# Input projection of a diffusion backbone step: kept row parts, weight splits moved from GpSimd, and conditioning vectors computed on TensorE between projection steps

## What is computed

```python
mod = silu(c) @ w_mod + b_mod            # c for latent rows, c_ctx for context rows; w_mod 2048 x 12288
sh1, sc1, g1, sh2, sc2, g2 = split(mod, 6)                 # six vectors of 2048, for each of the two kinds of row
h = rmsnorm(x, norm1_g) * (1 + sc1) + sh1
p = h @ w_in                                               # 2048 x 4608
dq, dk, dv, gq, gk, gv = split(p)                          # differential heads, grouped-query heads
gq, gk = rmsnorm(gq, qn_g), rmsnorm(gk, kn_g)              # then rotary positions on latent rows of dq, dk, gq, gk
o = concat(diff_attention(dq, dk, dv), gqa(gq, gk, gv))    # latent rows read 128 cached rows too
x = x + g1 * (o @ w_out)                                   # 2048 x 2048
h2 = rmsnorm(x, norm2_g) * (1 + sc2) + sh2
x = x + g2 * experts(h2)                                   # 16 experts, top-k rows each, SwiGLU 2048 -> 1024 -> 2048
y = rmsnorm(x, final_norm_g)
```

## Time and profile before

| | us |
|---|---|
| median of 3 runs (2669.41 to 2671.88) | 2670.93 |
| the profiled execution, its own time | 2671.9 |
| its span, first to last instruction | 2669.8 |
| conditioning | 0 to 106.6 |
| turn-over | 106.6 to 119.9 |
| input projection | 119.9 to 876.4 |
| values' loads, until the first score | 876.4 to 882.6 |
| attention | 882.6 to 1205.6 |
| start of the output projection | 1205.6 to 1211.1 |
| output projection | 1211.1 to 1459.5 |
| norm, routing, gathering | 1459.5 to 1533.3 |
| experts | 1533.3 to 2629.7 |
| end | 2629.7 to 2669.8 |

### The profile page before, as it was taken

The page is one execution under the profiler, slowest core; times in us unless marked ns, Lnnn a source line. Parts: engine busy times, 40 slices in busy tenths (PEclk is TensorE's granted clock), DMA queues, the critical chain, the costliest instruction groups (busy, mean ns, idle before and its releaser), DMA issues.

```text
span 2669.8 us, 28206 instructions
## 1 busy us (share of the span) xinstructions
PE 2252.4 (84%) x10506; PEld 1573.5 (59%) x10506; DVE 2007.6 (75%) x1696; ACT 1226.3 (46%) x1293; POOL 873.8 (33%) x396
## 2 busy tenths in 40 slices
PE   3777866887788788878999299999999999999994
PEld 0256645665566556657777266666666666666662
DVE  1177899998983477774322599999999998889895
ACT  1233322232223333323210277777777776666773
POOL 1297967899996000000000001111111111222221
PEclk8698988898988899978999599999999999999997
DMA  9753433346431200004212899999999999999996
GB/s 380 292 189 122 143 128 133 136 143 213 173 126 64 97 1 1 1 1 160 79 64 89 303 354 376 380 381 379 382 380 384 384 384 384 380 379 379 378 390 235
DMA packets 207807, 623.78 MB, mean 234 GB/s; under 512 B 10745, under 2 KB 12281, under 8 KB 172233
## 3 DMA queue, kind: packets, MB, share of 16 engines
q1 hardware_dynamic: 194880, 557.88, 56.1%
q0 software_dynamic: 6496, 35.51, 4.9%
q10 hardware_dynamic: 6352, 29.36, 2.9%
HBM read 593.15 MB, written 29.62 MB: 233 GB/s over the span
## 4 chain that ended last, share of the span: by engine, by line
PE 56%; DVE 21%; DMA 9%; POOL 8%; issue 3%; ACT 2%; SPq 0%; ACTq 0%; DVEq 0%; POOLq 0%; PEldq 0%
PE ps L505 16%; PE ps L506 16%; PE ps L507 16%; DVE arena L1451 7%; POOL B_x_lo L1226 4%; POOL B_w_lo L1227 3%; DMA arena<-in_w_mod 3%; DMA arena<-in_w_expert_down 3%; DVE arena L1415 2%; PE ps L766 2%; DVE mx L1465 2%; DVE arena L1417 2%; PE ps L732 2%; DVE arena L1410 1%; ACT arena L1065 1%
## 5 line engine op out<-in xcount | busy, mean ns | idle before, releaser
L1165 ACT ACTIVATE E_w_hi<-arena 128x2048 fp32r<-128x2048 f32 x384 | 735.9, 1917 | 282.2 <-PE ps L507 170.4
L1655 DVE TENSOR_TENSOR E_w_lo<-arena,E_w_hi 128x2048 fp32r<-128x2048 f32 x256 | 579.4, 2287 | 71.5 <-ACT E_w_hi L1165 70.3
L1304 POOL DMA_INDIRECT acc_d<-arena,idxC x16 | 181.9, 11371 | 764.1 <-DVE arena L1698 764.1
L1451 DVE SCALAR_TENSOR_TENSOR arena<-arena,cT 128x2048 f32<-128x2048 f32 x120 | 393.9, 3321 | 38.2 <-DMA arena<-in_w_mod 33.4
L505 PE MATMUL ps<-E_w_hi,E_xsT_hi 128*80 128x512 f32 x1024 | 405.9, 396 | 13.1 <-DVE E_w_lo L1655 13.1
L1226 POOL TENSOR_TENSOR B_x_lo<-arena,B_x_hi 128x640 fp32r<-128x640 f32 x144 | 362.5, 2520 | 165.3 <-ACT B_w_hi L965 151.4
L506 PE MATMUL ps<-E_w_hi,E_xsT_lo 128*80 128x512 f32 x1024 | 403.4, 394 | 0.0
L1655 DVE TENSOR_TENSOR E_w_lo_late<-arena,E_w_hi 128x2048 fp32r<-128x2048 f32 x128 | 291.9, 2287 | 14.6 <-ACT E_w_hi L1165 13.8
L507 PE MATMUL ps<-E_w_lo,E_xsT_hi 128*80 128x512 f32 x768 | 300.0, 391 | 0.0
L507 PE MATMUL ps<-B_w_lo,B_x_hi 128*128 128x512 f32 x720 | 293.2, 407 | 0.0
L505 PE MATMUL ps<-B_w_hi,B_x_hi 128*128 128x512 f32 x360 | 154.3, 429 | 106.2 <-POOL B_w_lo L1227 105.4
(11 more groups left out here) (215 smaller groups left out, 3755.0 us busy)
## 6 DMA issues: line engine op xcount, KB each, us to landing
arena<-in_w_expert_gate SPq DMA_DIRECT2D x128, 1024.0 KB, 14.2
arena<-in_w_expert_up SPq DMA_DIRECT2D x128, 1024.0 KB, 14.4
arena<-in_w_expert_down SPq DMA_DIRECT2D x128, 1024.0 KB, 17.4
arena<-in_w_mod SPq DMA_DIRECT2D x96, 1024.0 KB, 5.6
arena<-in_w_in SPq DMA_DIRECT2D x36, 1024.0 KB, 5.7
arena<-in_w_out SPq DMA_DIRECT2D x16, 1024.0 KB, 5.0
arena<-in_x_sample ACTq DMA_DIRECT2D x8, 1024.0 KB, 11.7
acc_d<-arena POOLq DMA_DIRECT2D x1, 5120.0 KB, 18.9
```

Of the source, the lines that this page charges most:

```text
L1165: act.activation(split_e(j)[0][:, :], at(slot_e(j), D), ACT.Copy).then_inc(xw_hi, 1)
L1304: pool.indirect_dma_start(acc_d[:, :], bass.IndirectOffsetOnAxis(ap=idxC[:, e:e + 1], axis=0), xrow_out[0:CAP, :], None, compute_op=ALU.ad ...
L1451: ins = dve.scalar_tensor_tensor(out=maccs[m][v], in0=w, scalar=cT[:, k, v:v + 1], in1=maccs[m][v], op0=ALU.mult, op1=ALU.add)
L1655: dve.tensor_tensor(w_lo[:, :], at(slot_e(j), D), w_hi[:, :].bitcast(F32), ALU.subtract).then_inc(xw_lo, 1)
```

## The change

ORDER becomes 8, 2, 3, 4, 0, 1, 6, 7, 5. The row parts `x_hi` and `x_lo` of all sixteen channel pieces are computed once and stay in memory ("xsplit": four activations on ScalarE, L1045, two of which apply scale and shift with rounding and two in place, and one subtraction on VectorE, L1442). The weights are split in halves of a chunk (128x1024, two steps; 72 halves): `w_hi` by ScalarE (L1038) in a ring of three, `w_lo` by VectorE (L1438) in place of the raw weights. GpSimd computes nothing there but two small powers; it issues DMAs. All 96 chunks of `w_mod` go through TensorE (L721, `cT` padded with zeros to 32 columns): 32 in the first stage, where c and c_ctx are now the first transfers of SyncE's queue and the row transposes (L706, L709) and their plain copies (L1022) stand between the chunks, and 64 between the steps of the projection, where `MOD_AT` puts them, through a ring of two. The sums over partitions, `selv`, the accumulators and "cols2" are gone; a finished vector is copied out of its bank (L1031) and turned by four transposes (L697).

The V loads go to SyncE's queue, issued after step 11 of the last block. `x` is loaded again once the scores are done. The output projection is split by halves too (`HI_D` = 3 halves, before 3 chunks), and the residual of a block comes before the next split on VectorE. Eleven of the first twelve expert chunks are issued ahead of the wait for `acc_stored`, before eight. The memory layout changes with all this. Attention, routing and the expert loop are as before.

```diff
-ORDER = [8, 6, 7, 2, 3, 4, 0, 1, 5]
+ORDER = [8, 2, 3, 4, 0, 1, 6, 7, 5]
...
-MOD_PACE = [(2, 3, 3, 3), (0, 2, 3, 3), (0, 1, 3, 3), (0, 1, 3, 3), (0, 2, 3, 3), (1, 2, 2, 3), (2, 2, 3, 3), (0, 1, 2, 2)]
+TEN, NINE = (0, 2, 3, 5, 6, 8, 10, 11, 13, 14), (0, 2, 4, 5, 7, 9, 11, 12, 14)
+MOD_AT = [(1, 3, 5, 7, 9, 11, 13, 15), TEN, TEN, NINE, NINE, NINE, NINE, (), ()]
...
+                elif kind == "mod":
+                    n = step[1]
+                    where, s, fill = mod_slot(n)
+                    mi, k = n // KC, n % KC
+                    if n == 0:
+                        pe.wait_ge(c_ready, 1)
+                    elif k == 0:
+                        pe.wait_ge(mod_copied, mi)
+                    pe.wait_ge(mod_landed[s], 16 * fill)
+                    w = at(where, 4, NB)
                     for c in range(4):
-                        mm = pe.matmul(bank(4 * m + c)[32 * c:32 * c + 2, :], cT[:, k, :], w[:, c, :], start=(k == 0),
-                                       stop=(k == KC - 1))
+                        mm = pe.matmul(bank(5)[32 * c:32 * (c + 1), :], cT[:, k, :], w[:, c, :], start=(k == 0),
+                                       stop=(k == KC - 1), skip_group_check=True)
+                    mm.then_inc(mod_used if k < KC - 1 else mod_done, 1)
                 elif kind == "projk":
...
-                    pe.wait_ge(pb_lo, n_k + 1)
+                    if k % 2 == 0:
+                        pe.wait_ge(w_lo_ready, u + 1)
+                    if o == 0:
+                        pe.wait_ge(x_lo_ready, k + 1)
...
+                elif kind == "split":
+                    u = step[1]
+                    raw, w_hi, _ = half_b(u)
+                    if u >= HI_B:
+                        after_products(act, (u - HI_B) // 8, 2 * ((u - HI_B) % 8) + 1)
+                    act.wait_ge(w_landed[u // 2 % RING_B], 16 * (u // 2 // RING_B + 1))
+                    act.activation(w_hi, raw, ACT.Copy).then_inc(w_hi_ready, 1)
+                elif kind == "xsplit":
+                    k = step[1]
+                    if k == 0:
+                        act.wait_ge(A1_ready, 1)
+                    for dst in (parts_B["x_hi"][k], xT[:, k, :]):
+                        for v, cols in ((0, slice(0, LAT)), (1, slice(LAT, TOK))):
+                            ins = act.activation(dst[:, cols], xT[:, k, cols], ACT.Identity, bias=modT[:, 0, v, k:k + 1],
+                                                 scale=A1[:, v, k:k + 1])
+                    ins.then_inc(x_hi_ready, 1)
...
-            def low_parts(n):
-
-                (x, w), (x_hi, w_hi), (x_lo, w_lo) = split_b(n)
-                pool.wait_ge(pb_hi, n + 1)
-                pool.tensor_tensor(x_lo, x, x_hi.bitcast(F32), ALU.subtract)
-                pool.tensor_tensor(w_lo, w, w_hi.bitcast(F32), ALU.subtract).then_inc(pb_lo, 1)
...
+                elif kind == "split":
+                    u = step[1]
+                    raw, w_hi, w_lo = half_b(u)
+                    dve.wait_ge(w_hi_ready, u + 1)
+                    dve.tensor_tensor(w_lo, raw, w_hi.bitcast(F32), ALU.subtract).then_inc(w_lo_ready, 1)
```

897 lines of the change are left out of this document (430 added, 467 removed).

## The result

The changed kernel takes 2478.91 us (median of four runs, 2475.09 to 2480.68) for 2671.4 of the kernel before: a ratio of 0.928, with an interval of 0.926 to 0.930. That is 192.5 us less, where 174 were forecast, and lies inside the range of 2466 to 2550. The profiled execution took 2480.0 us, with a span of 2478.2.

The account below looks back on a forecast made before the run. GpSimd was taken to end last in the projection, with TensorE waiting for `w_lo`. 2671.9 - 0.8 - 160.1 - 5.2 - 2.0 - 1.9 - 4 = 2497.9 us; range 2466 to 2550, 0.84.

Parts of the forecast that it names:

- So GpSimd ends last there: Projection: TensorE waits for `w_lo` from GpSimd 52 times, 155.4 us, so GpSimd was taken as the last engine.
- The clock's rival: Projection: 64 switches keep the clock low, total 2550 at 0.92; chance 0.17, shared with a dearer way there and back.
- the rival of late splits: Projection: each of 35 chunk borders costs TensorE 3 us, +105, total 2603; chance 0.08, with landings late in part.
- the 226 us beside the L1451: Projection: VectorE's 620 us less 394 for conditioning vectors, taken as shaping within a forecast load of 325 us.
- The row of the sum: First-stage distance of 2.54 us around a sum, giving 0.39 us for the way there and back, 1.24 a chunk.
- Boundaries and cold start of the projection: Projection: 3 us for first steps at the low clock, 8 for eight block boundaries and short clock falls.
- I take 4 us off (0 to 8): First stage: c and c_ctx loaded first shorten the gap before the first matmul, which had waited until 24.4 us.
- counted with 6 and 5 us: First stage: 6 us exposed for row transposes between chunks, 5 for two `w_in` chunks ahead of the last `w_mod` ones.
- The tail behind the last chunk: First stage's end: copy, four transposes, A1, one row split and its `x_lo`, about 5.5 us; before, 13.3.
- the wait for V: Attention: V loads start four steps earlier, so a wait of 1.98 us at 895.27 goes, -2.0; bound: it stays.
- The reason given: Output projection: clock of 0.98 is worth 5 us; smaller splits and the residual's new place may give most, -4.
- the experts are bound by TensorE, and no row shows it waiting for the first ones: Before the experts: issuing expert chunks early was counted as 0, bound -5.

Follow-up runs that it names:

- the ring of one: The changed kernel with one buffer instead of two for the projection's `w_mod` chunks; 2521.5 us, the projection 628.8 us.
- The pairs: The changed kernel with the projection's 64 conditioning chunks in 32 pairs, two at every place; 2464.09 us.
- The version with another first stage: The changed kernel with one row piece behind each of chunks 12 to 27 and `w_in` loaded behind the last `w_mod` chunk; 2469.47 us.
- The version with the late residual: The changed kernel with the fifth row tile's transposes and copy behind a block's last output-projection product, and the residual behind them; 2491.81 us.

## Why the prediction was right, and where it was off

**What bounds the kernel: right in the main, but not the whole chain.** The waits are gone, TensorE's products come every 0.227 us, and the clock stayed at 1.00. "So GpSimd ends last there" holds for 82 of the 155.4 us; the other 73 began with a `w_in` chunk that stood in the queue behind a `w_mod` chunk, for which VectorE had not freed the buffer. The prediction named only the first. That the same edits removed both was luck in so far as it was not argued. The clock's rival, which had the largest chance beside the forecast, did not happen: 64 ways to another kind of matmul and back left the granted clock at 1.00 over the whole stage. Among dense products it was seen to fall behind true waits, as with the ring of one, and in the kernel before once at a block boundary of the output projection (below). Nor did the rival of late splits: ScalarE does stand for the landing of each of the 36 chunks of `w_in`, 276.4 us in all, but the splits are far enough ahead that TensorE waits for none of them.

**The load of VectorE: much too high, without harm.** The prediction took the 226 us beside the L1451 over as shaping, though some 15 of them are L1449 and L1433. Without these three lines the window of the kernel before has 216 us of shaping. After, the window has 177 us in all, 84 of them for 69 halves of weights and 12 for `x_lo`, so some 80 us of shaping. With `w_lo` on GpSimd it is some 103. It had named the rule of the Trainium skill (SBUF — State Buffer, Who interferes with whom) by which a two-input instruction of VectorE contends with GpSimd's reads, and said that the shaping would shrink; the rows bear this out in both directions, and the shrunk figure should have gone into the sum. One pair of rows sets the two kinds of instruction side by side: the product of 128x512 with itself (two inputs) took 1830 ns in the kernel before (L1380) and 690 in the changed one (L1332), while the sum over the same 128x512 (TENSOR_REDUCE, one input; L1381, L1333) took 686 ns in both.

**The chunks: 79.2 us forecast, 76.7 measured (64 x 1.20).** The row of the sum was the right neighbour. The pairs show that the 0.34 us beyond the rate are paid once for a way there and back, as the rule of the Trainium skill (TensorEngine Tiling (Array Packing), Key Properties) says of a change of the mode; no run here shows whether it is a drain. What the prediction missed is that a group of row transposes next to a chunk costs less, 0.38 instead of 0.45 us, and 14 of the 35 groups stand there; and that five of the 35 are only half as long. All that stands between the products costs 91.3 us, not 95.7.

**Boundaries and cold start of the projection: 11 us forecast, 5.2 measured** (586.2 - 489.7 - 91.3). Together these two terms are the 10.2 us from 596.4 to 586.2, and with them the 9.8 us of the table, where the stage before is 756.1 and not 756.5.

**The start: its sum was near, by two errors that cancel.** The step that failed is "I take 4 us off (0 to 8)" for the gap ahead of the first chunk. TensorE multiplies its first chunk at 12.1 us for 26.5, but the transfers came no sooner: the DMA moved 14.1 MB in the first 40 us before and 14.2 after (its rates, by 10 us, 315, 288, 399, 411 and 312, 292, 409, 403 GB/s), and TensorE waits for the fifth chunk until 36.8 us before and 37.5 after:

```profile
36.82 1.88 PE L672 MATMUL ps<-arena,cT 128*2 128x512 f32 x8 [4.47 <-DMA arena<-in_w_mod]
...
37.45 1.93 PE L721 MATMUL ps<-arena,cT 128*32 128x512 f32 x8 [2.10 <-DMA arena<-in_w_mod]
```

On the other side, the row pieces and the two chunks of `w_in` had been counted with 6 and 5 us; the last chunk of the stage ended at 106.5 us before and at 111.7 to 117.2 in the seven executions with the new first stage, so together they cost 5 to 11. The version with another first stage ends its last chunk at 107.1 us: both delays can be had back, and nothing of the 4 us appears even there. The tail behind the last chunk was right (5.5 us forecast, 5.1 to 5.5 measured). The forecast of 119.1 us lies inside the 116.8 to 122.7 measured; the 3.5 us of the table are no more than this scatter, of which the execution explained here is the latest.

**The way to the output projection: -9.1 forecast, -10.7 measured.** The first score was right (-5.2 forecast, -5.4 measured, 1.3 us behind the last product), and so was the output projection's own start (-1.9 forecast, -1.8 measured). The table's windows, 5.50 and 5.33 us, do not show the latter since their left ends stand at different instructions. Inside attention -2.0 were forecast for the wait for V, which is gone, and -3.5 measured, with the scatter named above.

**The output projection: -4 forecast, -4.2 measured.** The reason given holds. In the kernel before the clock fell once, behind the boundary of the second and third blocks, where TensorE had two tiles of transposes and small matmuls and waited for banks:

```profile
1325.00:1340.00 15.00, 13.75 (x57) 9.71 (x56) 10.41 (x13) 5.53 (x11) 0.00 (x0) 0.77 0.21 71
```

0.77 over 15 us is some 3.4 us of the 4.2; in the changed kernel the clock is 1.00 from 1095 us to the stage's end. The version with the late residual shows that it is the residual's new place that keeps it there, and not the smaller splits.

**Before the experts: 0 forecast, -9.5 measured.** The failed step is "the experts are bound by TensorE, and no row shows it waiting for the first ones". I asked only whether the chunks are late, not what they collide with. Three to four microseconds come from the gathering that no longer shares the DMA with four chunks, which undoing the edit shows (3.7); some 5.5 from the last residual, which starts ahead of the last product, of which undoing the edit shows 3.7. Both stood in the trace before: a wait of 12.5 us for the gathered rows, and VectorE idle until TensorE had finished.

## What to carry to other kernels

When an engine is last by a wide margin, several edits can each take away most of its excess, and their gains overlap; price them in the order in which they are made, and ask which pair makes the waits vanish. A wait is put down to the engine that ended last, which may itself have stood still: look at its own idle time just before the longest waits, and follow it back to the queue. Small matmuls in another form between dense ones pay their way there and back once for a group: put such work in groups as large as the buffers allow. A transfer moved earlier is also a transfer taken from beside something else: look for what runs next to it, in both places.

## What the runs showed of the hardware

The same VectorE shaping took some 216 us beside a busy GpSimd, about 103 beside one with 69 subtractions, and about 80 beside an idle one, while its one-input sums over 128x512 kept their 0.69 us; GpSimd's subtraction of 640 columns took 2.52 us beside a VectorE with 119 two-input instructions of 2048 columns and 1.74 beside one whose same instructions had 8 columns.

TensorE's granted clock was 1.00 over 586 us of products with 64 fp32 chunks in between. After a wait of 3.7 us it was at the low level, and a chunk lasted 1.94 instead of 1.07 us.

An fp32 chunk of four matmuls in groups of 32 columns between dense products cost 1.20 us alone and 2.06 as a pair: 0.86 for each and 0.34 once. A group of four fp32 transposes cost 0.45 us there, and 0.45 us is also the difference of its distance at the two levels of the clock (0.44 and 0.89 us).
